# Products for R, K and V of an fp32 recurrence kernel: eight block products per pair of output columns, or seven

## The reference, cut to what matters

```python
def rwkv7_time_mix(xn, mu, w_in, w0, w1, w2, a0, a1, a2, ...):
    x_prev = jnp.pad(xn, ((0, 0), (1, 0), (0, 0)))[:, :-1]
    xmix = xn[None] + (x_prev - xn)[None] * mu[:, None, None, :]
    rkvg = jnp.einsum('cbsd,cde->cbse', xmix[:4], w_in)      # R, K, V, G: four 512x1024x1024 products
    r, k, v, g = rkvg[0], rkvg[1], rkvg[2], rkvg[3]
    xw, xa = xmix[4], xmix[5]
    w_pre = (w0 + jnp.tanh(xw @ w1) @ w2).astype(f32)        # inner width 64
    a = jax.nn.sigmoid((a0 + (xa @ a1) @ a2).astype(f32))    # inner width 64
    ...
```

## Time and profile before

| | |
|---|---|
| median of three runs | 2797.6 us (2796.61 to 2799.96) |
| the profiled execution | 2795.23 us |
| span of its trace | 2793.9 us |
| TensorE busy | 2630.1 us, 94% of the span |
| VectorE busy | 1057.3 us, 38% |
| ScalarE busy | 706.3 us, 25% |
| the stage that the change touches | from 1651 to 1893 us |
| in it, from R's first product to the first of G | 1651.1 to 1836.3 us |

### The profile page before, as it was taken

One profiled execution on the slowest core, in us unless ns is written; L12 is line 12 of the kernel. 1 busy time (PEld: TensorE's weight loads), 2 busy tenths in 40 slices (PEclk: granted clock), 3 DMA queues, 4 the chain that ended last, 5 costly groups with the idle time before them and its releaser, 6 DMA issues. The chain is left out here.

```text
span 2793.9 us, 41682 instructions
## 1 busy us (share of the span) xinstructions
PE 2630.1 (94%) x17040; PEld 1548.0 (55%) x17040; DVE 1057.3 (38%) x2301; ACT 706.3 (25%) x1148; POOL 166.1 (6%) x128
## 2 busy tenths in 40 slices
PE   8999999999999899898999879999999998999997
PEld 3666766344445667565665534447787444555533
DVE  4666565422213222222222151115776224444422
ACT  2233332100003111111111111235554213344421
POOL 0000000000000022222222200000000000000000
PEclk9999999999999899999999989999999999999999
DMA  6222211333331689999898833331111211111110
GB/s 263 106 91 76 91 68 37 114 136 135 135 132 76 264 319 369 390 338 397 314 398 322 294 151 109 128 147 52 49 49 56 111 63 55 61 56 51 46 53 30
DMA packets 81997, 428.11 MB, mean 153 GB/s; under 512 B 16240, under 2 KB 16752, under 8 KB 39184
## 3 DMA queue, kind: packets, MB, share of 16 engines
q1 hardware_dynamic: 53872, 368.47, 33.5%
q0 software_dynamic: 18096, 37.80, 5.3%
q10 hardware_dynamic: 9840, 19.17, 1.9%
HBM read 394.88 MB, written 58.79 MB: 162 GB/s over the span
## 5 line engine op out<-in xcount | busy, mean ns | idle before, releaser
L281 PE MATMUL psum_all<-u,weights 128*128 128x512 f32 x976 | 425.7, 593 | 0.0
L281 PE MATMUL psum_all<-big,weights 128*128 128x512 f32 x704 | 308.9, 596 | 7.1 <-DVE big L986 6.4
L281 PEld LDWEIGHTS psum_all<-u,weights 128*128 128x128 f32 x976 | 183.6, 190 | 219.4 <-issue 219.0
L281 PEld LDWEIGHTS psum_all<-big,weights 128*128 128x128 f32 x704 | 134.5, 191 | 177.2 <-issue 176.2
L2052 PE MATMUL psum_all<-big,weights 128*128 128x512 f32 x512 | 224.5, 598 | 6.1 <-DVE big L2167 4.9
L1525 PE MATMUL psum_all<-big 128*32 128x256 f32 (+2 forms) x1648 | 197.0, 387 | 9.9 <-DMA big<-t_experts 8.4
L1525 PE MATMUL psum_all<-weights,big 128*64 128x256 f32 (+2 forms) x1296 | 191.4, 398 | 10.3 <-DMA weights<-t_experts 10.0
L2052 PEld LDWEIGHTS psum_all<-big,weights 128*128 128x128 f32 x512 | 97.0, 191 | 132.9 <-issue 127.4
L1525 PEld LDWEIGHTS psum_all<-big 128*32 128x32 f32 (+2 forms) x1648 | 138.2, 134 | 44.7 <-issue 14.0
L1525 PEld LDWEIGHTS psum_all<-weights,big 128*64 128x64 f32 (+2 forms) x1296 | 132.9, 148 | 52.3 <-issue 17.4
L281 PE MATMUL psum_all<-weights,u 128*128 128x256 f32 x640 | 139.6, 379 | 0.0
(11 more groups left out here) (396 smaller groups left out, 3370.7 us busy)
## 6 DMA issues: line engine op xcount, KB each, us to landing
big<-t_experts SPq DMA_DIRECT2D x96, 1024.0 KB
weights<-t_experts SPq DMA_DIRECT2D x96, 1024.0 KB
weights<-t_ada SPq DMA_DIRECT2D x24, 1024.0 KB, 6.9
weights<-t_rkvg SPq DMA_DIRECT2D x16, 1024.0 KB, 7.9
rwkv_inputs<-big ACTq DMA_DIRECT2D x48, 256.0 KB, 2.0
big<-rwkv_inputs SPq DMA_DIRECT2D x8, 1280.0 KB, 6.8
weights<-t_x SPq DMA_DIRECT2D x8, 1024.0 KB, 5.2
weights<-t_BC SPq DMA_DIRECT2D x8, 1024.0 KB, 4.9
```

The costliest lines, as they stand in the source:

```text
L281: last = pe.matmul(out, lhsT, rhs, start=n == 0, stop=n == len(terms) - 1)
```

## The change

Ten pieces of two columns (R's columns 4 to 7, all of K, all of V) are made with Strassen's scheme in Winograd's form. The product of a piece is split in two by two: the tokens into halves of 256, the sum over `k` into halves of four blocks, and the piece into its two columns. Seven block products P1 to P7 of four products each, with 256 tokens, take the place of eight. The differences that the scheme needs are made by VectorE: of the mix once for each of R, K and V (`rows_dve`, three new blocks of 128x1024 and one in place), of the weights for each piece (`columns_dve`, three new blocks of 128x512 and one in place in the weight slot). The results are put together by two copies on ScalarE (`seven_act`: P1 and P5 into `sq`) and five additions on VectorE (`seven_dve`); the `C11` quarter is summed in PSUM and copied by ScalarE. A piece uses three PSUM banks, and pieces take turns between banks 0 to 2 and 3 to 5. `X.columns` has two sets of differences, so those of piece n+2 are made when piece n is done.

Two more things move. The second stage of W and A no longer follows V's columns one `j` at a time: `SMALL_AFTER` puts `j` = 0, 1, 2 behind V's second piece, 3, 4, 5 behind the third and 6, 7 behind the fourth, in banks 6 and 7. And the mixes stand at other places: W and V together behind piece 1, A behind piece 5, G behind the first stage of W and A. R's first four columns and G are computed as before.

```diff
--- before.py
+++ after.py
-        self.BIG = 28000
+        self.BIG = 28160
...
+class Rows:
+    def __init__(self, src, extra):
+        n = src.shape[1] // 2
+        self.a11, self.a21, self.a12, self.a22 = src[:, 0:n, 0:HALF], src[:, 0:n, HALF:T], src[:, n:2 * n, 0:HALF], src[:, n:2 * n, HALF:T]
+        self.s1, self.s2, self.s4 = extra
+        self.s3 = self.a21
+class Columns:
+    def __init__(self, b1, b2, extra):
+        n = b1.shape[1] // 2
+        self.b11, self.b21, self.b12, self.b22 = b1[:, 0:n, :], b1[:, n:2 * n, :], b2[:, 0:n, :], b2[:, n:2 * n, :]
+        self.t1, self.t2, self.t4 = (e.rearrange("p (k m) -> p k m", m=P) for e in extra)
+        self.t3 = self.b12
...
+class Seven:
+    def __init__(self, K, banks):
+        self.banks = a, b, c = banks
+        self.r1 = K.psum[:, a, 0:HALF]
+        self.r4, self.r6 = K.psum[:, b, 0:HALF], K.psum[:, b, HALF:T]
+        self.r7, self.r5 = K.psum[:, c, 0:HALF], K.psum[:, c, HALF:T]
+def rows_dve(K, q, key, R, src_read=None):
+    dve, tt = K.nc.vector, K.nc.vector.tensor_tensor
+    tt(R.s1, R.a21, R.a22, ALU.add).then_inc(*q.dve.tick())
+    dve.wait_ge(*q.dve.now())
+    tt(R.s2, R.s1, R.a11, ALU.subtract).then_inc(*q.dve.tick())
+    dve.wait_ge(*q.dve.now())
+    tt(R.s4, R.a12, R.s2, ALU.subtract).then_inc(*q.dve.tick())
+    if src_read is not None:
+        dve.wait_ge(*src_read)
+    tt(R.s3, R.a11, R.a21, ALU.subtract).then_inc(*q.dve.tick("rows", key))
+def columns_dve(K, q, n, B):
+    tt = K.nc.vector.tensor_tensor
+    tt(B.t1, B.b12, B.b11, ALU.subtract).then_inc(*q.dve.tick())
+    K.nc.vector.wait_ge(*q.dve.now())
+    tt(B.t2, B.b22, B.t1, ALU.subtract).then_inc(*q.dve.tick())
+    tt(B.t3, B.b22, B.b12, ALU.subtract).then_inc(*q.dve.tick())
+    K.nc.vector.wait_ge(*q.dve.now())
+    tt(B.t4, B.b21, B.t2, ALU.subtract).then_inc(*q.dve.tick("columns", n))
+def part(pe, out, w, x, first=True):
+    n = w.shape[1]
+    for k in range(n):
+        ins = pe.matmul(out, w[:, k, :], x[:, k, :], start=first and k == 0, stop=k == n - 1, skip_group_check=not first)
+    return ins
+def seven_pe(K, q, n, R, rows_event, B, Z, r1_read):
+    pe = K.nc.tensor
+    K.bank(Z.banks[0], *r1_read)
+    part(pe, Z.r1, B.b11, R.a11).then_inc(*q.pe.tick("P1", n))
+    pe.wait_ge(*q.dve.at("columns", n))
+    K.bank(Z.banks[1], q.dve, "c21", n)
+    part(pe, Z.r4, B.t4, R.a22).then_inc(*q.pe.tick("P4", n))
+    pe.wait_ge(*rows_event)
+    K.bank(Z.banks[2], q.dve, "c12", n)
+    part(pe, Z.r7, B.t3, R.s3)
+    part(pe, Z.r5, B.t1, R.s1).then_inc(*q.pe.tick("P5", n))
+    part(pe, Z.r6, B.t2, R.s2).then_inc(*q.pe.tick("P6", n))
+    pe.wait_ge(*q.act.at("p1", n))
+    part(pe, Z.r1, B.b21, R.a12, False).then_inc(*q.pe.tick("P2", n))
+    pe.wait_ge(*q.act.at("p5", n))
+    return part(pe, Z.r5, B.b22, R.s4, False)
+def seven_act(K, X, q, n, Z, p1_read, p5_read):
+    act = K.nc.scalar
+    act.wait_ge(*q.pe.at("P1", n))
+    if p1_read is not None:
+        act.wait_ge(*p1_read)
+    act.activation(X.p1, Z.r1, ACT.Copy).then_inc(*q.act.tick("p1", n))
+    act.wait_ge(*q.pe.at("P5", n))
+    if p5_read is not None:
+        act.wait_ge(*p5_read)
+    act.activation(X.p5, Z.r5, ACT.Copy).then_inc(*q.act.tick("p5", n))
+def seven_dve(K, X, q, n, Z, done, c21, c22, c12):
+    dve, tt = K.nc.vector, K.nc.vector.tensor_tensor
+    dve.wait_ge(*q.act.at("p1", n))
+    dve.wait_ge(*q.pe.at("P6", n))
+    tt(c12, Z.r6, X.p1, ALU.add).then_inc(*q.dve.tick("g", n))
+    dve.wait_ge(*q.dve.now())
+    dve.wait_ge(*done)
+    tt(c22, Z.r7, c12, ALU.add).then_inc(*q.dve.tick())
+    dve.wait_ge(*q.dve.now())
+    tt(c21, Z.r4, c22, ALU.add).then_inc(*q.dve.tick("c21", n))
+    dve.wait_ge(*q.act.at("p5", n))
+    dve.wait_ge(*q.dve.now())
+    tt(c22, c22, X.p5, ALU.add).then_inc(*q.dve.tick("c22", n))
+    tt(c12, Z.r5, c12, ALU.add).then_inc(*q.dve.tick("c12", n))
...
+SEVENS = [(R_, 2), (R_, 3)] + [(K_, m) for m in range(4)] + [(V_, m) for m in range(4)]
+FIRST_V = SEVENS.index((V_, 0))
+SMALL_AFTER = {1: (0, 1, 2), 2: (3, 4, 5), 3: (6, 7)}
+STORES = [(c, j) for c in (R_, K_) for j in range(KD)] + \
+    [key for m in range(4) for key in [(V_, 2 * m), (V_, 2 * m + 1)] + [(c, j) for j in SMALL_AFTER.get(m, ()) for c in (W_, A_)]] + \
     [(G_, j) for j in range(KD)]
...
-        self.mix = {R_: second, K_: third, W_: first, A_: second, V_: third, G_: first}
+        self.mix = {R_: second, K_: third, W_: first, A_: third, V_: second, G_: first}
         self.small = K.carve(T)
+        self.columns = [in_three(K.carve(3 * T)) for _ in range(2)]
+        extras = [in_three(K.carve(6 * T), HALF) for _ in range(2)]
+        self.rows = {c: Rows(self.mix[c], extras[n]) for c, n in ((R_, 0), (K_, 1), (V_, 0))}
+        self.p1, self.p5 = K.sq_both[:, 0:HALF], K.sq_both[:, HALF:T]
+        self.sets = [Seven(K, (0, 1, 2)), Seven(K, (3, 4, 5))]
...
+    def seven(n):
+        c, m = SEVENS[n]
+        w = w0 + LOAD_AT[c] + m
+        pe.wait_ge(*K.W.here(w))
+        if c != R_:
+            pe.wait_ge(*q.dve.at("mix", c, KD - 1))
+        seven_pe(K, q, n, X.rows[c], q.dve.at("rows", c), inputs_unit(K, X, w0, n), X.sets[n % 2], (q.act, "c11", n)) \
+            .then_inc(*K.W.left(w, q.pe))
+
+    for n in range(2):
+        pe.wait_ge(*K.W.here(w0 + n))
+    for j in range(4):
+        K.bank(j % 4, q.act, "out", R_, j)
+    for k in range(KD):
+        pe.wait_ge(*q.dve.at("mix", R_, k))
+        for j in range(4):
+            product(R_, j, k)
+    for n in range(FIRST_V + 1):
+        seven(n)
...
     w = w0 + SECOND_AT
-    for j in range(KD):
-        column(V_, j)
-        if j == 0:
+    for m in range(1, 4):
+        seven(FIRST_V + m)
+        if m == 1:
             pe.wait_ge(*K.W.here(w))
             for c in (W_, A_):
                 pe.wait_ge(*q.act.at("small", c))
-        for n, c in enumerate((W_, A_)):
-            K.bank(5 + n, q.act, "out", c, j)
-            pe.matmul(K.psum[:, 5 + n, :], K.W.slots[w % K.W.N][half(n), j * P:(j + 1) * P], X.small[half(n), :],
-                      start=True, stop=True) \
-                .then_inc(*(q.pe.tick("out", c, j) if (c, j) != (A_, KD - 1) else K.W.left(w, q.pe)))
+        for j in SMALL_AFTER[m]:
+            for n, c in enumerate((W_, A_)):
+                K.bank(6 + n, q.act, "out", c, j)
+                pe.matmul(K.psum[:, 6 + n, :], K.W.slots[w % K.W.N][half(n), j * P:(j + 1) * P], X.small[half(n), :],
+                          start=True, stop=True) \
+                    .then_inc(*(q.pe.tick("out", c, j) if (c, j) != (A_, KD - 1) else K.W.left(w, q.pe)))
     for j in range(KD):
...
+    def seven(n):
+        c, m = SEVENS[n]
+        Z, i = X.sets[n % 2], STORE_AT[c, 2 * m]
+        seven_act(K, X, q, n, Z, q.dve.at("g", n - 1) if n else None, q.dve.at("c22", n - 1) if n else None)
+        act.wait_ge(*K.out_stored[i % 4].at(*STORES[i - 4]))
+        act.wait_ge(*q.pe.at("P2", n))
+        act.activation(X.out[i % 4][:, 0:HALF], Z.r1, ACT.Copy).then_inc(*q.act.tick("c11", n))
+        act.wait_ge(*q.act.now())
+        act.wait_ge(*q.dve.at("c21", n))
+        act.dma_start(scratch[2 * m, :, STORED[c], :], X.out[i % 4]).then_inc(*K.out_stored[i % 4].tick(c, 2 * m))
+        act.wait_ge(*q.dve.at("c22", n))
+        act.wait_ge(*q.dve.at("c12", n))
+        act.dma_start(scratch[2 * m + 1, :, STORED[c], :], X.out[(i + 1) % 4]).then_inc(*K.out_stored[(i + 1) % 4].tick(c, 2 * m + 1))
+
+    for j in range(4):
+        evict(R_, j, j % 4, ACT.Copy)
+    for n in range(FIRST_V + 1):
+        seven(n)
...
+    for m in range(1, 4):
+        seven(FIRST_V + m)
+        for j in SMALL_AFTER[m]:
+            evict(W_, j, 6, ACT.Sigmoid, K.col("a_w0_2", j))
...
+    def columns(n):
+        c, m = SEVENS[n]
+        dve.wait_ge(*K.W.here(w0 + LOAD_AT[c] + m))
+        if n >= 2:
+            dve.wait_ge(*seven_event(q, w0, n - 2))
+        columns_dve(K, q, n, inputs_unit(K, X, w0, n))
+
+    def seven(n):
+        c, m = SEVENS[n]
+        i = STORE_AT[c, 2 * m]
+        for other in (i, i + 1):
+            dve.wait_ge(*K.out_stored[other % 4].at(*STORES[other - 4]))
+        even, odd = X.out[i % 4], X.out[(i + 1) % 4]
+        seven_dve(K, X, q, n, X.sets[n % 2], seven_event(q, w0, n), even[:, HALF:T], odd[:, HALF:T], odd[:, 0:HALF])
+
     dve.wait_ge(*before.act.at("next rstd"))
     normed(0)
     for k in range(KD):
@@ -2176,21 +2346,40 @@
         mixed(R_, k)
     for k in range(KD):
         mixed(K_, k)
+    columns(0)
+    columns(1)
+    rows_dve(K, q, R_, X.rows[R_], q.pe.at("w", w0 + LOAD_AT[R_] + 1))
+    dve.wait_ge(*q.dve.at("mix", K_, KD - 1))
+    rows_dve(K, q, K_, X.rows[K_])
     dve.wait_ge(*before.act.at("final rstd"))
     for k in range(KD):
         dve.scalar_tensor_tensor(K.h[:, k, :], K.h[:, k, :], K.col("final_norm_g", k), K.rstd[:, :], ALU.mult, ALU.mult) \
             .then_inc(*q.dve.tick())
-    for k in range(KD):
-        mixed(W_, k)
```

(80 more changed lines are left out.)

15 lines of the change are left out of this document (4 added, 11 removed).

## The result

The changed kernel takes 2808.1 us (median of 20 runs, 2801.4 to 2825.9) beside 2798.4 us for the kernel before in the same sessions: a ratio of 1.0041, with a 95% interval of 1.0031 to 1.0051, that is 8.7 to 14.3 us slower. Run again beside later experiments the ratio was 1.0033 (1.0021 to 1.0046). The forecast was 2796.0 us, with a range of 2786 to 2803. The executions of one kernel differ among themselves, the longer ones at a lower mean granted clock (the changed kernel's: 2801.4 us at 0.972, 2825.9 us at 0.964), and a trace is of one execution, so that what follows is read from stretches of the traces and not from whole spans. The profiled execution of the changed kernel has a span of 2803.3 us against 2793.9.

A forecast was written before the change was run, and what follows sets the result against it. TensorE, busy for 94% of the span, was taken to bound the kernel. 15.8 + 1.0 + 1.2 - 12.9 - 0.5 = 4.6 us gained, 1.6 with the clock, gave 2796.0 us, range 2786 to 2803.

The forecast's parts named there:

- The pieces: Ten two-column pieces on TensorE: 12.16 us each with seven block products in place of 13.74, 15.8 us less.
- The groups' waits: W's and A's second stage: three groups wait for ScalarE, 21.35 us against 8.4, so 12.9 us lost.
- The clock: At the pauses in W's and A's three groups: TensorE's clock falls, 3.0 us lost, with ends 0 and 5.2.
- Slower: the clock falls for longer: Rival at the three groups: short products between pauses hold the clock at half twice as long, 10.5 us lost; chance 0.10.
- Piece 3: P2 of piece 3 waits for ScalarE's copy of P1, which waits for VectorE's first addition of piece 2: 0.5 us lost.
- VectorE otherwise, and the transfers: VectorE's other new work is hidden beside the pieces, and weight loads come in time: transfers costed at nothing.

The follow-up runs named there:

- filled kernel: The changed kernel with 4, 2 and 2 extra unused products in the first pauses of W's and A's groups: 2795.3 us, ratio 0.9991 against the kernel before.
- kernel with the grouping alone: The kernel before, with eight plain block products and only W's and A's second stage put in groups of three, three and two: 2813.8 us, ratio 1.0060.
- the one with the lump moved: The changed kernel with V's mixes and row differences on VectorE behind piece 2 in place of piece 1: 2801.4 us, ratio 1.0014 against the kernel before.

## Why the prediction was wrong

The mechanism was seen and put in its place: groups that wait for their banks, and a clock that falls there. The clock's term was sized far too small, and a smaller term too. Point by point:

- **The pieces: right.** 12.16 us were forecast, 12.08 measured. Ten pieces gave 0.8 us more than forecast.
- **The groups' waits: right.** The first waits were forecast at 3.4, 2.1 and 2.1 us and measured at 3.33, 2.05 and 2.05. At full clock, which the filled kernel shows, the groups take 8.95, 7.7 and 5.4 us, 22.0 in all (0.2 of it because the extra products outlast the first pause); 21.35 were forecast. The table load cost 1.29 us to its sigmoid (1789.85 to 1791.14), as in the earlier trace rows.
- **The clock: the step that failed.** "I take 3.0, with ends 0 and 5.2." Changed kernel less the same work at full clock: 26.08 - 22.05 = 4.0 us in the groups, 2.0 in piece 8, 2.2 in piece 9 (14.49 us; 12.29 is the filled kernel's piece 8, its own piece 9 has a fall in it and takes 13.87), 2.1 in G's first columns. That is 10.3 us in place of 3.0, twice the upper end. Two assumptions were wrong. Each fall was given one stretch of 3.5 us, as at the earlier trace rows's 1651.5, where dense products followed the pause; here the stretches at 0.50 were 10.2, 10.2 and 6.8 us, 27 us together in place of 7. And the two later pauses, of 2.05 us, were given a fall in half of the cases, by pauses of 1.94 and 2.23 us in the earlier trace rows; both pauses had one, in both traces of the changed kernel. The length of the pause alone was looked at, not the half-width products with waits between them that follow it here. The runs show that such work comes ahead of falls and lies in the long ones; which trait of it counts, the half width or the waits, they do not separate.
- **The rival that described it.** "Slower: the clock falls for longer" had the price, 10.5 us, nearly exactly, and 0.10 of the chance. That it came so near is in part luck: it counts 7 us at half clock for each group, 21 in all, where 27 were measured, some of them under waits for ScalarE. What I held against it, the recurrence with its many small pauses at 1.00, was a stretch in which TensorE is busy for 90% of the time; in the first group it had worked for 1.05 of 4.45 us. Even so the objection does not part the cases, since in the filled kernel TensorE was busy for 4.20 of the 4.30 us ahead of its fall. The Trainium skill ("TensorE: Matmul & The Clock Gate", section "A second HAM failure mode: psum-queue depth-cycling") says that frequent small pauses between groups of products make the clock go back and forth. By that the changed kernel's trace agrees, with three falls to 0.50 at its groups, and the recurrence at 1.00 does not.
- **Piece 3: mis-sized.** 0.5 us forecast, 2.37 measured. The step had P2 wait for the copy of P1, and the copy for VectorE's first addition of piece 2. VectorE came to that addition as forecast, at 1725.06 (1725.3). The step left out that on ScalarE this copy also stands behind piece 2's two stores, and these wait for the last addition:

```profile
1727.35 0.33 ACTq L2278 DMA_DIRECT2D rwkv_inputs<-big  x1
1727.78 0.38 ACT L980 ACTIVATE sq<-psum_all 128x256 f32<-128x256 f32 x1 [11.81 <-DVE big L1001]
```

- **VectorE otherwise, and the transfers: right.** No wait of TensorE for VectorE or a load appears in the stage.

The sum with the measured sizes is 18.0 + 0.8 - 13.6 - 2.4 - 10.3 = -7.5 us; the stage, from R's first product to the recurrence, is 8.0 us longer, and G's first column starts at 1842.33 where 1833 to 1835 was forecast. Of the other 0.5 us, 0.2 lie in R's first four columns, which took 29.6 us where 29.4 were taken: the clock was at 0.50 there from 1648.5 to 1655.3, in the kernel before from 1651.5 to 1655.0. The kernel with the grouping alone, which is the same program as the kernel before at that place, has the longer stretch too (1650.0 to 1656.7), so it is not put down to the change. The last 0.3 us have no place.

## What to carry to other kernels

When an edit takes products away, ask first what had to move to make room: here small products whose evictions had been hidden came to stand in groups, in which nearly each waits for its bank. Spread such products through the dense ones, a full eviction apart; the same seven-product pieces then gave 0.45% in place of a loss of 0.4%, and 0.7% with V's mixes moved as well. And when TensorE's waits are priced, price the clock over the whole stretch of half-width, waiting work behind the pause and into the dense products after it, not over the pause.

## What the runs showed of the hardware

The granted clock stayed at 0.50 for 10.2 us with TensorE at work in 10.12 of them: 6.1 us of half-width products that each waited for a bank, then the first dense products of the next piece. In the changed kernel's two traces and in the one with the lump moved it fell within a microsecond of the end of each group's first pause (2.05 to 3.33 us, nine falls). Twice it fell at no such pause but behind 3.3 us (grouped) and 4.3 us (filled) of such products at 1.00. With dense extra products in the pause, results unused, the first group ran at 1.00, and the kernel with such fillings became 0.4 to 0.5% faster.
